# Bias tables of the last mixer issued by another queue, their mask added at another place, and other places at which TensorE waits for turned tiles

## What is computed

```python
def peer_ffn(x, wq, keys, u, v):            # 8 heads x 16 picked rows = 128 rows a token
    ...
    act = gelu(einsum('td,thkd->thk', xb, u[ib])) * gb
    return einsum('thk,thkd->td', act, v[ib])

def second_block(x, ...):                   # the third block of the whole
    h = rms_norm_2(x, g_mix)
    qa, ka, va, qd, kd, vd, qm = split(h @ w_in)
    # 8 heads: 2-D neighbourhood attention, bias from na_rpb, a column window as a mask
    # 12 heads in 3 groups: dilated attention, bias from a T5 table
    # 4 heads: attention to a memory
    x = x + concat([out_na, out_dil, out_mem]) @ w_out
    return x + hierarchical_moe(rms_norm_2(x, g_ffn), ...)
```

## Time and profile before

| what | value |
|---|---|
| median of 3 runs | 2306.08 us (2305.84 to 2307.43) |
| the profiled execution's own time | 2306.09 us |
| its span, first to last instruction | 2304.3 us |
| busy: PE, DVE, ACT, POOL | 1789.9, 1298.3, 850.6, 659.1 us |
| moved by DMA | 920.49 MB, mean 399 GB/s |
| chain that ended last, by engine | DMA 48%, PE 32%, DVE 10%, ACT 6% |

### The profile page before, as it was taken

The page is one execution under the profiler, slowest core; times in us unless marked ns, Lnnn a source line. Parts: engine busy times, 40 slices in busy tenths (PEclk is TensorE's granted clock), DMA queues, the critical chain, the costliest instruction groups (busy, mean ns, idle before and its releaser), DMA issues.

```text
span 2304.3 us, 30881 instructions
## 1 busy us (share of the span) xinstructions
PE 1789.9 (78%) x11196; PEld 848.4 (37%) x11196; DVE 1298.3 (56%) x3217; ACT 850.6 (37%) x2292; POOL 659.1 (29%) x606
## 2 busy tenths in 40 slices
PE   9999877695797777588779666877779997766666
PEld 4655521161352343153336112343327553222222
DVE  4878887668757766866776867555442331111111
ACT  1324354444445544454744435444333520000000
POOL 1002444434433433533443444333322300000000
PEclk9999887696798888689989667888979999788888
DMA  9988799999999999999999999999999399999998
GB/s 395 381 351 347 314 420 421 420 420 419 388 421 421 421 421 421 421 382 421 412 410 421 421 420 421 421 421 420 421 404 333 121 392 422 428 428 429 428 428 372
DMA packets 111150, 920.49 MB, mean 399 GB/s; under 512 B 12806, under 2 KB 15140, under 8 KB 19044
## 3 DMA queue, kind: packets, MB, share of 16 engines
q0 software_dynamic: 76800, 549.70, 57.9%
q1 hardware_dynamic: 34212, 369.02, 38.8%
HBM read 917.57 MB, written 6.06 MB: 401 GB/s over the span
## 4 chain that ended last, share of the span: by engine, by line
DMA 48%; PE 32%; DVE 10%; ACT 6%; issue 3%; POOL 1%; SPq 0%; DVEq 0%; POOLq 0%; ACTq 0%
DMA arena<-in_peer_uv_dram,arena 27%; DMA arena<-in_moe_pieces_dram 14%; PE summed L1560 8%; DVE y_g L3153 4%; PE gp L1652 3%; PE gp L1105 3%; DMA mod<-in_w_parts_dram 3%; DMA arena<-in_w_slots_dram 2%; PE gp L1967 2%; PE gp L1110 2%; PE gp L1648 2%; DMA arena<-in_w_parts_dram 1%; PE gp L1781 1%; ACT arena L2311 1%; PE gp L1532 1%
## 5 line engine op out<-in xcount | busy, mean ns | idle before, releaser
L1560 PE MATMUL summed<-arena 64*64 64x512 f32 x4096 | 693.8, 773 | 338.5 <-ACT arena L2311 313.9
L3153 DVE CUSTOM_DVE_ANT_0 y_g<-arena,h 128x1024 f32<-128x1024 f32 x512 | 627.3, 1225 | 389.6 <-DMA arena<-in_peer_uv_dram,arena 332.1
L1036 POOL DMA_INDIRECT arena<-in_peer_uv_dram,arena x512 | 592.8, 1158 | 885.9 <-PE summed L1560 805.4
L1560 PEld LDWEIGHTS summed<-arena 64*64 64x64 f32 x4096 | 136.3, 157 | 760.3 <-ACT arena L2311 660.3
L2305 ACT ACTIVATE arena<-arena 128x1 f32<-128x1 f32 x512 | 102.7, 201 | 558.0 <-DVE arena L3153 556.9
L1967 PE MATMUL gp<-arena,mod 128*32 128x512 f32 x1008 | 156.5, 758 | 98.5 <-DMA arena<-in_moe_pieces_dram 98.5
L2311 ACT ACTIVATE arena<-cst,arena 128x128 f32<-128x128 f32 x512 | 205.5, 401 | 16.8
L3546 DVE TENSOR_TENSOR mod<-mod,gp 128x512 f32<-128x512 f32 x8 | 5.5, 687 | 353.7 <-ACT mod L2620 353.7
L2308 ACT ACTIVATE arena<-arena 128x1 f32<-128x1 f32 x512 | 150.8, 294 | 16.6
L1967 PEld LDWEIGHTS gp<-arena,mod 128*32 128x32 f32 x1008 | 31.7, 124 | 214.8 <-DMA arena<-in_moe_pieces_dram 156.8
L2620 ACT ACTIVATE mod<-gp 128x512 f32<-128x512 f32 x8 | 4.8, 597 | 246.7 <-PE gp L1967 246.7
(11 more groups left out here) (530 smaller groups left out, 2339.3 us busy)
## 6 DMA issues: line engine op xcount, KB each, us to landing
arena<-in_moe_pieces_dram SPq DMA_DIRECT2D x92, 2048.0 KB, 25.5
arena<-in_w_slots_dram SPq DMA_DIRECT2D x43, 2048.0 KB, 12.5
arena<-in_w_parts_dram SPq DMA_DIRECT2D x42, 1024.0 KB, 9.3
mod<-in_w_parts_dram SPq DMA_DIRECT2D x23, 1024.0 KB, 9.6
arena<-in_peer_uv_dram,arena POOLq DMA_INDIRECT x512, 15.7
t_rep<-t_rows POOLq DMA_DIRECT2D x1, 3066.0 KB, 18.3
arena<-t_rep POOLq DMA_DIRECT2D x1, 2304.0 KB, 12.8
ext<-in_w_parts_dram SPq DMA_DIRECT2D x2, 1024.0 KB, 22.8
```

Source lines behind the costliest of these rows:

```text
L1036: pool.indirect_dma_start(rowbuf[b], None, a["peer_uv"].rearrange("l n d -> (l n) d"), bass.IndirectOffsetOnAxis(ap=idx[:, col(n):col(n) + ...
L1560: mm = pe.matmul(op[o:o + HALF, b, :], diag[i:i + HALF, n % DIAGS, i:i + HALF], rowbuf[n % ROWS][i:i + HALF, D + b * 512:D + (b + 1) * 512 ...
L3153: v.tensor_tensor_reduce(y[:, t, :], rowbuf[n % ROWS][:, 0:D], h[:, t, :], 1.0, 0.0, ALU.mult, ALU.add, dots[:, c:c + 1]).then_inc(udot, 1)
```

## The change

Three things move, and one instruction is added.

1. SP issues the 17 bias tables behind the first four slots of `in2`, ahead of the other slots, where POOL issued them after the last gather. The semaphore is `loaded` in place of `bias_in`.
2. DVE adds the mask ahead of the head norms: `mask_tables` is the first call of `last_attention`.
3. PE's three waits for the turned tiles in `second_layer` stand at the first reader (s = 9, 67, 84), not behind the transposes (s = 5, 64, 81).
4. ACT has one more square root of one column, written to a column that nobody reads, behind its last PEER row and ahead of the sums of squares.

```diff
@@ SP
             for n in range(phase_slots["in2"][0], phase_slots["in2"][0] + RING):
                 sync.wait_ge(vsum, rows_left(place[n]))
                 sync.dma_start(ring[:, place[n], :], a["w_slots"][n]).then_inc(w_landed[place[n]], 16)
+            sync.wait_ge(bias_w, 64)
+            sync.wait_ge(x_ready, 4 * T + 1)
+
+            sync.dma_start(dil_bias, bass.AP(tensor=t5_rep.tensor, offset=127, ...)).then_inc(loaded, 16)
+            W = NA_HEADS * NDR * RW
+            for hh in range(NA_HEADS):
+                for r2 in range(2):
+                    sync.dma_start(na_bias[r2 * GRID_W:(r2 + 1) * GRID_W, hh, :]..., ...).then_inc(loaded, 16)
             for n in range(phase_slots["in2"][0] + RING, len(slots)):
                 load_weights(n)
@@ POOL
             pool.wait_ge(x_ready, 4 * T + 1)
-            pool.dma_start(dil_bias, ...).then_inc(bias_in, 16)
-            W = NA_HEADS * NDR * RW
-            for hh in range(NA_HEADS):
-                for r2 in range(2):
-                    pool.dma_start(na_bias[...], ...).then_inc(bias_in, 16)
             load_gain(5, a["g_ffn_2"][0])
             divide_last()
@@ PE, second_layer
                     if s == 5:
                         pe.wait_ge(d_h, 2 * t + 1)
                         turn_tile(h, t)
+                    if s == 9:
                         pe.wait_ge(d_hT, 6 * t + 2)
...
                         turn_tile(y, t)
+                    if s == 67:
                         pe.wait_ge(d_hT, 6 * t + 4)
...
                         turn_tile(h, t)
+                    if s == 84:
                         pe.wait_ge(d_hT, 6 * t + 6)
@@ ACT
             rows_to(PICKS)
+            act.activation(small[:, 16:17], eps[:, 0:1], ACT.Sqrt)
             half_square(1, 0, x_ready, 4 * T)
@@ DVE
             def mask_tables():
-                v.wait_ge(bias_in, 16 * (NA_HEADS + 17))
+                v.wait_ge(loaded, 16 * (NLOADS + 20))
...
             def last_attention():
+                mask_tables()
                 head_inverse("block2", 0)
                 head_scale("block2", 0)
                 head_scale("block2", 1)
                 head_inverse("block2", 1)
-                mask_tables()
                 head_scale("block2", 2)
```

More of the change, by code:

```diff
@@ L873, in _ @@
                 sync.dma_start(ring[:, place[n], :], a["w_slots"][n]).then_inc(w_landed[place[n]], 16)
+            sync.wait_ge(bias_w, 64)
+            sync.wait_ge(x_ready, 4 * T + 1)
+            sync.dma_start(dil_bias, bass.AP(tensor=t5_rep.tensor, offset=127,
+                                             ap=[[12 * TW - 1, P], [TW, 12], [1, 384]])).then_inc(loaded, 16)
+            W = NA_HEADS * NDR * RW
+            for hh in range(NA_HEADS):
+                for r2 in range(2):
+                    sync.dma_start(na_bias[r2 * GRID_W:(r2 + 1) * GRID_W, hh, :].rearrange("p (j n) -> p j n", j=6),
+                                   bass.AP(tensor=na_rep.tensor,
+                                           offset=hh * NDR * RW + (1 - r2) * RW + GRID_W - 1,
+                                           ap=[[W - 1, GRID_W], [RW, 6], [1, GRID_W]])).then_inc(loaded, 16)
             for n in range(phase_slots["in2"][0] + RING, len(slots)):
@@ L1038, in _ @@
             pool.wait_ge(x_ready, 4 * T + 1)
-            pool.dma_start(dil_bias, bass.AP(tensor=t5_rep.tensor, offset=127,
-                                             ap=[[12 * TW - 1, P], [TW, 12], [1, 384]])).then_inc(bias_in, 16)
-            W = NA_HEADS * NDR * RW
-            for hh in range(NA_HEADS):
-                for r2 in range(2):
[L1045 to L1048, removed]
             load_gain(5, a["g_ffn_2"][0])
```

## The result

The changed kernel takes 2313.47 us (median of 8 runs, 2310.85 to 2318.34), the kernel before 2307.26 us in the 8 runs beside it (2305.84 to 2310.80): ratio 1.0031, 95% interval 1.0021 to 1.0040. It is slower by 0.3%: 6.2 us by the medians, 7.2 by the ratio. Its profiled execution took 2312.98 us, with a span of 2311.2 us.

A forecast was written before the change was run, and what follows sets the result against it. DMA transfer at about 421 GB/s was taken as the bound, with losses behind three turned tiles. From 2306.09 us, -2.13, -2.14 and -1.43 make -5.7, all else 0: 2300.4 us, range 2297.2 to 2305.0.

The forecast's parts named there:

- The fifth slot: Last mixer: SP's fifth weight slot, behind the tables, lands at 1744.8, before PE wants it at 1745.97; cost 0.
- second rival: Last mixer: the fifth slot arrives late; half speed for small pieces gives 6 us back, 2306.4; chance 0.12.
- The waits at the readers: Turned tiles in second_layer: PE starts ready rows sooner; first -2.13, fourth -2.14, fifth -1.43, others 0; together -5.7 us.
- third rival: PEER rows: DMA engines take the gain back, transfer being lost for another reason than PE's pause; 0 to -2.9; chance 0.15.
- the loss there can pay all of it: First turned tile: 3.3 us of lost transfer covers PE's 2.13 us earlier start, so all 2.13 is gained.
- no `hT` wait remains, the copy is covered by the rows between: second_layer: ACT's 2.90 us copy ends while PE adds four rows, 5.32 us at the first tile.
- the mask fits into DVE's idle time: Last mixer: the mask runs from 1740 to 1744 on DVE, ahead of the first reciprocal at 1747.18; cost 0.
- the root and the gains' load bring nothing: Last mixer: the root takes a 1.28 us table load off the norm's way; gains' load some 45 us sooner; 0.
- first rival: Last mixer: tables land as late as before and hold the head norms; first spread waits 11.1 us, 2311.5; chance 0.07.
- PEER rows that end where they did: Sign against the forecast, in second_layer; it expected the last PEER row 5 to 6 us sooner.
- a wait of PE for a weight slot: Sign against the forecast, in the last mixer; it expected PE to go from slot to slot without a pause.
- a quarter of 5.57 us: Range's lower end: 1.5 us more if the second, third and sixth turned tiles, put at 0, bring a quarter.

The follow-up runs named there:

- two DMAs: The changed kernel with the window tables loaded by two DMAs of 768 KB instead of sixteen of 96 KB: 2309.77 us, ratio 1.0015 to the kernel before.
- The long pieces: The changed kernel with each window table reading 384 numbers in one row instead of six rows of 64: 2307.15 us, ratio 1.0001 to the kernel before.
- the tables alone: The kernel before with only the bias tables on SP and the early mask, without moved waits or added root: 2312.47 us, ratio 1.0025.
- three forms: Against the kernel before: moved waits only, 1.0001; with the added root, 0.9997; with the root and only the large table on SP, 0.9995.

## Why the prediction was wrong

**The fifth slot: the step that failed.** I wrote that however long SP takes to issue 17 tables, the slot is behind their bytes, which end at 1737.8, and lands at 1744.8 with 1.2 us to spare. Each half was wrong.
- *The rate.* I took the time of the tables from POOL's queue, as a share of all DMA engines. As work that share was about right in the change: 0.49 MB in 2.4 us are 203 GB/s, and on SP's queue 149 GB/s at a share of 0.76 are 196 (with two DMAs it was not: 111 at 1.00). But a share becomes time only if something else fills the rest, or the queue fills it itself. Before, slots ran on SP's queue beside POOL's tables. In the change all is one queue, the share falls to 0.48 to 0.79 while SP places a table in 0.67 us or is held once more, and fifteen tables take the 16 us from 1723.9 to 1740.0 where I had 7.2.
- *The issue.* "However long SP takes" left out that a slot that is issued late lands late: 1739.99 + 8.23 = 1748.2. The first table alone was held 9.00 us behind the slots and the large table's 1536 pieces; that the issuing engine can be held like this I had not considered. The Trainium skill (DMA: Bandwidth & Descriptors, section "Issuing engines are not separate DMA queues") has the issue as usually small beside the transfer. These sixteen issues differ, with 25.09 us of SP.
- *What a pause costs.* My second rival put 6 us on half the speed for the pieces, a stall of PE only. In the three profiles with all tables ahead of the fifth slot and the large one first, the stall is 3.83 to 5.06 us, and 1.6 to 2.9 us come on top, since PE runs the next products at the lower clock. That the rival's 6 us are near the measured loss is luck: it had neither the late issue nor the clock.

The long pieces settle which property of the tables does it: the same bytes, the same sixteen issues, a sixth of the pieces, no loss. A single issue of 2.36 MB in pieces of 1536 bytes did no harm either.

**The waits at the readers: -5.7 us, measured none.** The third rival, to which I gave 0.15, has the outcome right, but not its cause: it put the holes behind the tiles down to something else than PE's pause. The waits went, and the windows behind the tiles filled (144 GB/s became 406, 218 became 387). Windows of the changed kernel:

```profile
615.00:620.00 5.00, 5.00 (x48) 3.90 (x47) 3.54 (x11) 2.07 (x7) 1.26 (x2) 1.00 1.00 406
750.00:755.00 5.00, 4.60 (x36) 1.78 (x32) 4.39 (x11) 2.53 (x6) 2.93 (x3) 0.90 0.98 370
770.00:775.00 5.00, 1.99 (x8) 0.31 (x8) 4.57 (x13) 4.09 (x8) 2.16 (x3) 0.64 0.93 375
990.00:995.00 5.00, 5.00 (x45) 3.54 (x42) 3.49 (x10) 2.30 (x8) 2.78 (x3) 1.00 1.00 387
```

The two in the middle had 419 and 418 before. Over windows of 5 us from 560 to 1710, the time lost against 421 GB/s is 15.2 us before and 17.0 with the tables alone; with the moved waits alone it is 14.5, and in the two profiles of the change 13.8 and 15.0. The most that this leaves is a microsecond or two, not 5.7: the holes moved. Where the gain goes can be followed on PE behind the first tile. The kernel before:

```profile
609.91 1.97 PE L1632 MATMUL turned<-cst,h 128*128 128x128 f32 x8
...
698.76 1.94 PE L1668 MATMUL turned<-arena,cst 128*64 128x512 f32 x8
...
708.97 1.47 PE L1560 MATMUL summed<-arena 64*64 64x512 f32 x8 [2.65 <-ACT arena L2311]
710.37 0.80 PE L1679 MATMUL scores<-arena 64*128 64x128 f32 x4
```

and the changed one:

```profile
607.90 1.97 PE L1634 MATMUL turned<-cst,h 128*128 128x128 f32 x8
...
693.14 1.94 PE L1670 MATMUL turned<-arena,cst 128*64 128x512 f32 x8
...
701.60 1.08 PE L1670 MATMUL turned<-arena,cst 128*64 128x512 f32 x4 [2.32 <-DVE arena L3262]
...
704.64 1.09 PE L1562 MATMUL summed<-arena 64*64 64x512 f32 x8 [0.94 <-ACT arena L2316]
708.45 1.09 PE L1562 MATMUL summed<-arena 64*64 64x512 f32 x8 [2.72 <-ACT arena L2316]
709.46 0.49 PE L1681 MATMUL scores<-arena 64*128 64x128 f32 x4
```

Counted from the turned tile, where the changed kernel is already 2.0 us ahead, PE has won 3.6 us at the first spread of the head norms and has lost all of it and 1.5 us more at the row before the first head's scores. In between it waits for DVE and for ACT's diagonals, and DVE in turn for rows that have not landed:

```profile
694.90 1.23 DVE L3159 CUSTOM_DVE_ANT_0 y_g<-arena,h 128x1024 f32<-128x1024 f32 x1 [1.16 <-DMA arena<-in_peer_uv_dram,arena]
...
699.56 1.22 DVE L3159 CUSTOM_DVE_ANT_0 y_g<-arena,h 128x1024 f32<-128x1024 f32 x1 [2.13 <-DMA arena<-in_peer_uv_dram,arena]
```

Over longer stretches the other profiles show the same. With the wait at the reader the first part begins 6.8 to 6.9 us behind the first tile's transposes (eleven profiles), with the wait behind the copy 9.4 (two); yet from the first tile's transposes to the second's it is 169.8 to 172.3 us in the one case and 170.2 and 170.8 in the other, and from the first tile's transposes to the last PEER row 1100.1 to 1102.8 against 1101.5 and 1103.0. A mean of 0.9 us may have stayed; with two profiles on one side that isn't shown.

The step that failed here was "the loss there can pay all of it". I read each hole as time lost for good, and didn't ask whether the stretch behind it could use an earlier start. The full rate of the slices behind it, 421, was the warning: PE reached rows that the DMA engines, full as they were, had not delivered. Which instruction sets the length of that stretch between the heads, where the new holes are, the runs don't isolate.

**Right:** no `hT` wait remains, the copy is covered by the rows between, the mask fits into DVE's idle time, the root and the gains' load bring nothing that can be told, and the first rival's price (11.1 us forecast, 12.12 measured by itself). But "PEER rows that end where they did" and "a wait of PE for a weight slot", named as what would prove me wrong, both came. Two smaller slips: a quarter of 5.57 us is 1.4, where the range took 1.5; and that the mask at its old place costs nothing was read from one execution, while three of the five profiles with that place show a wait of PE for it (1.16 to 3.32 us).

**No better version.** The moved waits without the tables on SP, in three forms, stand at 1.0001, 0.9997 and 0.9995 of the kernel before, each with an interval that holds 1: as fast as before, not faster. The part to leave out is the sixteen small tables on SP.

## What to carry to other kernels

Where a queue feeds the critical path, its issuing engine can come onto that path: before something is moved in front of it, count the DMAs and the pieces, since a row from another queue prices neither. A wait that is taken away in front of a stretch that already runs at the full transfer rate can return as another wait inside it; the distance between two landmarks that enclose both tells sooner than the hole itself.

## What was not expected of the hardware

- The same tables are 2.1 KB packets from POOL's queue and 256-byte packets from SP's: 6145 more under 512 bytes. The Trainium skill (DMA: Bandwidth & Descriptors, section "SWDGE vs HWDGE vs iDMA") describes packets of preferably at most 4096 bytes for the queue that GpSimd feeds. These 2.1 KB agree; the 576 packets of the large table with one window table, 2.46 MB, are 4.3 KB each and lie a little above.
- SP itself can stand still at an issue for microseconds: 9.00 us for the first window table behind four slots and the large table's 1536 pieces, 6.10 behind one slot and these, 7.22 and 5.91 for the fourth window table behind four slots and 1152 pieces. That its queue was full then is my reading; no row shows how much the queue holds.
- An issue of a window table takes SP 0.62 to 0.70 us when it isn't held, and 0.60 with a sixth of the pieces; a slot of 2 MB then takes 0.33 and the large table 0.38. Why, no run tells.
- Pieces of 256 bytes can fill the DMA engines at rates far below the 421 GB/s of the PEER rows: 111 GB/s at a share of 1.00 and 198 at 1.16, in two successive windows of one run.
